# First feed-forward's gate/up with joined 512-column products over four PSUM banks

## The chip, the cores and the metric

The kernel runs on one core of one Trainium2 chip. The metric is the time of one execution on the device in microseconds (us), the lower the better.

## What is computed

Two transformer-like blocks follow each other. The first block works on 256 tokens of 1024 features: a mixer, then a gated feed-forward, then a small gate with a projected side input. The second block has two layers with conditioned norms; their scales and shifts come from a condition vector times a large matrix (`ada_w`). The stretch that matters here is the feed-forward of the first block, and beside it the condition product:

```python
h = rmsnorm(x, ffn_pre_norm[i])
f = (jax.nn.silu(h @ w_ffn_gate[i]) * (h @ w_ffn_up[i])) @ w_ffn_down[i]
x = x + rmsnorm(f, ffn_post_norm[i])

mod = jax.nn.silu(cond) @ w + b        # w is ada_w of either layer, for two conditions
```

Gate and up have 2816 columns each (22 tiles of 128). The same feed-forward stands in both layers of the second block, with the weights `ffn_w_gate_up` and `ffn_w_down`.

## The kernel before

Products are computed to more than the precision of one pass: every weight and every activation is split into a rounded high part and the low part that is left. With activations `xh`, `xl` (two halves of one tile, `xhl`) and weights `wh`, `wl`, a product is the sum of three matmuls: high by high, high weight by low activation, low weight by high activation.

Weights stream in units of 512 KB (`raw`, four slots). A unit passes four stations. SyncE's queue (SP) starts its transfer (`load`, L399) once GpSimd has finished with the unit four before it. ScalarE writes the high part `wh` (`high`, L649). GpSimd (POOL) writes the low part `wl` (`low`, L559). TensorE (PE) multiplies (`features`). Two units are one step, and a step of a gate/up phase gives one tile of gate and one tile of up. So there are 22 steps, numbered 0 to 21 below.

The gate/up phase of the first block is called `gu`. Its step alternates between pair 0 (bank 0) and pair 1 (bank 1); gate and up share a bank, 256 columns each. For every one of the 8 feature tiles, of both outputs, `three` (L1083 to L1085) issues three matmuls of 256 columns. After a step, ScalarE takes the silu of the gate (`sil`, L895), VectorE multiplies it by the up half (`ft`, L1770) and so frees the banks, ScalarE writes the high part `fh` (L899), and VectorE the low part `fl` (L1774), which it announces with the semaphore `f_lo`. ScalarE makes the high parts of the next weights (`high_step`) after `fh`, both units of a step one behind the other.

Beside this, VectorE computes the condition product row by row (`condition`, L1621 and L1624: two passes over a row tile of 1024, one per condition vector). The condition vectors lie in banks 2, 3, 5 and 6 at that time. VectorE does a step's rows at the head of that step, ahead of the wait for its silu. In the first 14 steps (`GU_LOOP` = 7 turns of a hardware loop, two slots for row tiles) a step has one row. In the last 8 steps, which are unrolled, steps of pair 0 have two rows and steps of pair 1 have one (`GX_ROWS`; four slots). The row tiles (512 KB each, `load_ada`, L429) are started by SP too, in one queue with the weights and in a fixed order: in the loop two units, a row, two units, a row; in the last steps a unit, then unit and row by turns. A row's transfer waits until VectorE has used up the row that lay in its slot (`ada_used`, counted by L1624), and whatever stands behind it in SP's queue waits with it.

The last layer's gate/up phase, `gu1`, is of the same size (256 tokens, 22 steps), has no condition rows beside it, and is written with joined products. There `joined` multiplies `wh` by `xh` and `xl` side by side, 512 columns into a whole bank (L1089), and `wl` by `xh`, 256 columns into the bank's first half (L1090). Such a step fills two banks, 0 and 1 or 2 and 3. Its results are in two halves that must be added: ScalarE copies the second halves of both banks to SBUF (`sf`, L891), VectorE adds them to the first halves (L1767), and then silu and the rest follow. ScalarE's order differs too: behind the copy it makes the high part of the first unit of the step after next (`high_half`), and that of the second unit behind `fh`.

The phase `dn` (down) follows `gu`, with three products of 256 columns in banks 0 and 1 and three condition rows to each pair of outputs. Bank 4 (`rstd_ps`) and bank 7 (`sums_ps`, `acc_ps`, and the last piece of the side projection, `PP_BANKS`) are used around `gu`, not in it; `take_pp` (L872) copies that piece out of bank 7 during step 0.

```python
def joined(o, wa, wb, k):
    nc.tensor.matmul(o, wa, xhl[:, :, k, 0:SEQ], start=k == 0, stop=False, skip_group_check=True)
    return nc.tensor.matmul(o[:, SEQ:2 * SEQ], wb, xh[:, k, 0:SEQ], ...)
```

Of the kernel before, what the change touches and what calls it, by code (L numbers as in the profile page):

```python
# [10 lines left out]
ALU = mybir.AluOpType  # L11
# [96 lines left out]
ADA_WOVEN = {"out": (1, 2, 0, 2), "gu": (1, 2, 2, 2 * GU_LOOP), "gx": (3, 4, 2 + 2 * GU_LOOP, 3 * (PH["gu"].iters - GU_LOOP))}  # L108
OUT = (1, 3, 0, 2, 4, 5, 6, 7)
GX_ROWS = ((0, 1), (2,))  # L110
JOINED = ('gu1',)
IN_U = (0, 1, 4, 5, 2, 3, 6, 7)
_at = sum(ADA_WOVEN["gx"][2:])
for _n, _per, _slots in (("dn", 3, 3), ("gu0", 2, 2), ("dn0", 3, 2)):
# [35 lines left out]
def build(nc, wall, wada, cond, xin, pin, par, tab, tab_ret, tab_rope, tab_mask, rpb, out):  # L150
    with ExitStack() as ctx:
        sems = {}

        def S(name):
            if name not in sems:
                sems[name] = ctx.enter_context(nc.semaphore(name))
            return sems[name]
# [135 lines left out]
        def pair_banks(j, n, wide=False):  # L293

            if n == SEQ and wide:
                return ps[:, 2 * j:2 * j + 2, 0:SEQ]
            if n == SEQ:
                return ps[:, j, :].rearrange("p (a b) -> p a b", a=2)
            return ps[:, 2 * j:2 * j + 2, :]

        def tile_bank(j, o, n, wide=False):

            return ps[:, j, o * SEQ:o * SEQ + SEQ] if n == SEQ and not wide else ps[:, 2 * j + o, 0:n]
# [340 lines left out]
        def _(act):  # L644
# [236 lines left out]
            def gate_up(ph, n, f0):  # L881

                def body(i, ahead=0):
                    for j in range(2):
                        split = ph.name in JOINED
                        if j >= ahead and not split:
                            high_step(ph, i, j)
                        pair_done(act, ph, i, j)
                        act.wait_ge(S("f_lo"), i * 2 + (f0 + j + 1))
                        if split:  # L890
                            nc.scalar.activation(sf[:, :, j, SEQ:NT], ps[:, 2 * j:2 * j + 2, SEQ:NT], ACT.Copy)\  # L891
                                .then_inc(S(f"small_{ph.name}"), 1)
                            high_half(ph, i, j + 1, 0)
                            act.wait_ge(S(f"joined_{ph.name}"), i * 2 + (j + 1))
                        nc.scalar.activation(sil[:, j, 0:n], tile_bank(j, 0, n, split), ACT.Silu)\  # L895
                            .then_inc(S("silu_ready"), 1)
                        act.wait_ge(bank_free, i * 2 + (ph.pair0 + j + 3))
                        settled(act)
                        nc.scalar.activation(fh[n][:, i * 2 + j, :], ft[:, j, 0:n], ACT.Copy).then_inc(S("f_hi"), 1)  # L899
                        if split:  # L900
                            high_half(ph, i, j + 1, 1)
                if ph.name == "gu1":
                    second_step(ph)
                if ph.name != "gu0":
                    preload(ACT.Silu)
                body(0, 1)
                with act.Fori(1, ph.iters) as i:
                    body(i)
# [162 lines left out]
        def _(pe):  # L1071
# [5 lines left out]
            def banks_ready(ph, i, pair):  # L1077

                pe.wait_ge(bank_free, i * 2 + (ph.pair0 + pair + 1))
# [13 lines left out]
            def features(ph, n, a=xh, b=xl, ktiles=KT, fresh=None, wide=False, within=None, first=0):  # L1093


                def body(i):
                    for j in range(ph.body):
                        pair = j // ph.per_pair
                        if j % ph.per_pair == 0:
                            banks_ready(ph, i, pair)  # L1100
                        for half in range(2):
                            slot = unit_ready(ph, i, j, half)
                            k0 = 2 * HALF * (j % ph.per_pair) + HALF * half
                            for o in range(2):
                                c = slice(o * P, o * P + P)
                                if within and isinstance(i, int) and (i, j) == (0, 0) and (half, o) in within:
                                    within[half, o]()
                                for kk in range(min(HALF, ktiles - k0)):
                                    k = k0 + kk
                                    if fresh and o == 0 and pair == 0:  # L1110
                                        sem, n0, each = fresh
                                        pe.wait_ge(S(sem), n0 + each * (k + 1))
                                    if ph.name in JOINED:
                                        mm = joined(ps[:, 2 * pair + o, :], wh[:, slot, kk, c], wl[:, slot, kk, c], k)
                                        continue
                                    mm = three(tile_bank(pair, o, n, wide), wh[:, slot, kk, c], wl[:, slot, kk, c],
                                               a[:, k, 0:n], b[:, k, 0:n], k == 0 and (n == NT or wide or o == 0), k == ktiles - 1)
                            mm.then_inc(units_done, 1)
                if first:
                    body(1)  # L1120
                else:
                    run(pe, ph, body, ph.iters - 1 if within else 0)
# [408 lines left out]
        def _(dve):  # L1531
# [225 lines left out]
            def gate_up(ph, n, f0):  # L1757
                def body(i):
                    for j in range(2):
                        if ph.name == "gu" and isinstance(i, int):  # L1760
                            condition("gx", 0, 0, [3 * (i - GU_LOOP) + s for s in GX_ROWS[j]])
                        else:
                            condition(ph.name, i, j)
                        dve.wait_ge(S("f_lo"), i * 2 + (f0 + j + 1))
                        if ph.name in JOINED:
                            dve.wait_ge(S(f"small_{ph.name}"), i * 2 + (j + 1))
                            V.tensor_tensor(pair_banks(j, n, True), pair_banks(j, n, True), sf[:, :, j, SEQ:NT], ALU.add)\  # L1767
                                .then_inc(S(f"joined_{ph.name}"), 1)
                        dve.wait_ge(S("silu_ready"), i * 2 + (f0 + j + 1))
                        V.tensor_tensor(ft[:, j, 0:n], sil[:, j, 0:n], tile_bank(j, 1, n, ph.name in JOINED), ALU.mult)\  # L1770
                            .then_inc(bank_free, 1)
                        dve.wait_ge(S("f_hi"), i * 2 + (f0 + j + 1))
                        f1 = bass.ds(i * 2 + j, 1)
                        V.tensor_tensor(fl[n][:, f1, :].rearrange("p a b -> p (a b)"), ft[:, j, 0:n],  # L1774
                                        fh[n][:, f1, :].rearrange("p a b -> p (a b)").bitcast(F32),
                                        ALU.subtract).then_inc(S("f_lo"), 1)
                run(dve, ph, body, ph.iters - GU_LOOP if ph.name == "gu" else 0)
# [432 lines left out]
```

## Time and profile before

| | |
|---|---|
| three runs | 1431.72, 1435.49, 1435.63 us (median 1435.49) |
| the profiled execution | 1431.83 us, of which the span is 1430.0 us |
| PE busy | 1391.8 us (97%) |
| PE weight loads | 1229.0 us (86%) |
| GpSimd busy | 845.2 us (59%) |
| VectorE busy | 749.9 us (52%) |
| ScalarE busy | 617.3 us (43%) |
| mean traffic with HBM | 156 GB/s |

Times in the rows are counted from the start of the span. Phase `gu` runs from 141.2 to 269.4 us, `dn` from there to 333 us, and `gu1` from 1231 to 1357 us. The columns of a timeline row are the start, the length, the engine, the line with its operation and tiles, and in brackets how long the engine had been idle and what released it. Matmuls overlap, so that the distance between two starts is the rate and the length is not.

### The profile page before, as it was taken

To read this page: it belongs to the slowest core of one execution; us is meant where nothing else is said; L and a number is where in the kernel's file an instruction comes from. 1 tells how busy PE (TensorE), PEld (TensorE's weight loads), DVE (VectorE), ACT (ScalarE), POOL (GpSimd) and SP (SyncE) were. 2 spreads that over 40 slices of the span, in tenths; PEclk is the share of its full clock that TensorE was granted. 3 is DMA by queue.
4 is the path that set the end of the run, shared out by engine and by line. 5 is a ranking of instruction groups with operands and counts; after the bars stand their busy time and mean duration, and the time that the engine had idled before them with its cause. 6 is when DMAs were issued, how large, how long until landed. Compare 5 with 4: busy or idle time off the path is not lost.

```text
span 1430.0 us, 24910 instructions
## 1 busy us (share of the span) xinstructions
PE 1391.8 (97%) x8774; PEld 1229.0 (86%) x8774; DVE 749.9 (52%) x1350; ACT 617.3 (43%) x997; POOL 845.2 (59%) x420
## 2 busy tenths in 40 slices
PE   9999999999999998899999999999999999999998
PEld 8999999999888887687888888888888788888897
DVE  4987457655634556637655655432514383444411
ACT  5566544444524444624323223322331365555552
POOL 5756888897374576132444444544465443688895
PEclk9999999999899999999999999999999999999999
DMA  7744678894232222033655556553393101455563
GB/s 250 252 156 155 243 281 305 290 322 146 82 92 86 74 74 74 17 102 105 204 194 202 177 192 219 178 185 134 93 243 97 44 18 62 140 184 185 186 211 103
DMA packets 82988, 227.28 MB, mean 159 GB/s; under 512 B 23664, under 2 KB 29040, under 8 KB 82672
## 3 DMA queue, kind: packets, MB, share of 16 engines
q1 hardware_dynamic: 82480, 224.91, 46.9%
q10 hardware_dynamic: 448, 1.57, 0.4%
q8 instruction: 37, 0.61, 0.2%
q14 instruction: 23, 0.19, 0.0%
HBM read 222.26 MB, written 1.05 MB: 156 GB/s over the span
## 4 chain that ended last, share of the span: by engine, by line
PE 42%; issue 32%; POOL 21%; DVE 4%; DVEq 1%; ACT 1%; POOLq 0%; ACTq 0%
POOL wl L559 18%; PE ps L1083 7%; PE ps L1085 7%; PE ps L1084 7%; PE ps L1089 6%; PE ps L1090 3%; DVE ps L1808 2%; PE ps L1170 2%; PE ps L1184 1%; PE ps L1160 1%; PE ps L1161 1%; PE ps L1162 1%; PE ps L1472 1%; POOL xhl L579 1%; PE ps L1398 1%
## 5 line engine op out<-in xcount | busy, mean ns | idle before, releaser
L559 POOL TENSOR_TENSOR wl<-raw,wh 128x1024 fp32r<-128x1024 f32 x310 | 747.4, 2432 | 519.7 <-ACT wh L649 519.4
L1083 PE MATMUL ps<-xhl,wh 128*128 128x256 f32 (+1 forms) x1376 | 460.2, 334 | 6.9 <-POOL wl L559 1.8
L1084 PE MATMUL ps<-xhl,wh 128*128 128x256 f32 (+1 forms) x1376 | 454.8, 331 | 0.0
L1085 PE MATMUL ps<-xhl,wl 128*128 128x256 f32 (+1 forms) x1376 | 454.8, 331 | 0.0
L649 ACT ACTIVATE wh<-raw 128x1024 fp32r<-128x1024 f32 x310 | 321.1, 1054 | 273.7 <-PE ps L1085 187.8
L1083 PEld LDWEIGHTS ps<-xhl,wh 128*128 128x128 f32 x1376 | 262.3, 191 | 39.1 <-POOL wl L559 4.3
L1085 PEld LDWEIGHTS ps<-xhl,wl 128*128 128x128 f32 x1376 | 262.3, 191 | 23.9
L1084 PEld LDWEIGHTS ps<-xhl,wh 128*128 128x128 f32 x1376 | 262.4, 191 | 22.7
L1083 PE MATMUL ps<-fh,wh 128*128 128x256 f32 (+1 forms) x528 | 168.8, 320 | 0.6 <-POOL wl L559 0.6
L1085 PE MATMUL ps<-fh,wl 128*128 128x256 f32 (+1 forms) x528 | 168.6, 319 | 0.0
L1084 PE MATMUL ps<-fl,wh 128*128 128x256 f32 (+1 forms) x528 | 168.6, 319 | 0.0
L1089 PE MATMUL ps<-xhl,wh 128*128 128x512 f32 x352 | 125.1, 400 | 1.2 <-DVE xhl L1582 0.8
L1751 DVE SCALAR_TENSOR_TENSOR h<-ps,mod,h 128x256 f32<-128x256 f32 x48 | 20.3, 478 | 169.6 <-PE ps L1085 169.6
L1083 PEld LDWEIGHTS ps<-fh,wh 128*128 128x128 f32 x528 | 99.3, 188 | 9.1 <-POOL wl L559 1.0
L1085 PEld LDWEIGHTS ps<-fh,wl 128*128 128x128 f32 x528 | 99.3, 188 | 8.1
L1084 PEld LDWEIGHTS ps<-fl,wh 128*128 128x128 f32 x528 | 99.3, 188 | 8.0
L895 ACT ACTIVATE sil<-ps 128x256 f32<-128x256 f32 (+1 forms) x66 | 29.9, 452 | 161.1 <-PE ps L1085 161.1
L1090 PE MATMUL ps<-xhl,wl 128*128 128x256 f32 x352 | 98.8, 281 | 0.0
L1770 DVE TENSOR_TENSOR ft<-sil,ps 128x256 f32<-128x256 f32 (+1 forms) x66 | 33.6, 510 | 104.3 <-ACT sil L895 104.3
L1774 DVE TENSOR_TENSOR fl<-ft,fh 128x256 f32 (+2 forms) x66 | 57.9, 878 | 49.9 <-ACT fh L899 49.9
L1089 PEld LDWEIGHTS ps<-xhl,wh 128*128 128x128 f32 x352 | 66.1, 188 | 19.0 <-DVE xhl L1582 1.4
L1621 DVE SCALAR_TENSOR_TENSOR unread<-ada_late,ps 128x1024 bf16<-128x1024 f32 x56 | 68.3, 1219 | 11.3 <-DMA ada_late<-wada 7.5
(230 smaller groups left out, 1885.8 us busy)
## 6 DMA issues: line engine op xcount, KB each, us to landing
raw<-wall SPq DMA_DIRECT2D x310, 512.0 KB, 4.1
ada_late<-wada SPq DMA_DIRECT2D x56, 512.0 KB, 3.3
ada<-wada SPq DMA_DIRECT2D x40, 512.0 KB, 5.5
bias<-rpb SPq DMA_DIRECT2D x16, 256.0 KB, 7.4
sww<-qk SPq DMA_DIRECT2D x16, 128.0 KB, 2.4
h<-xin SPq DMA_DIRECT2D x1, 1024.0 KB, 6.4
csb<-cond SPq DMA_DIRECT2D x1, 1024.0 KB, 6.5
h<-xin SPq DMA_DIRECT2D x2, 512.0 KB, 5.4
```

The costliest lines, as they stand in the source:

```text
L559: nc.gpsimd.tensor_tensor(wl[:, slot, :, :], raw[:, slot, :, :], wh[:, slot, :, :].bitcast(F32), ALU.subtract).then_inc(lo_ready, 1)
L649: nc.scalar.activation(wh[:, slot, :, :], raw[:, slot, :, :], ACT.Copy).then_inc(hi_ready, 1)
L895: nc.scalar.activation(sil[:, j, 0:n], tile_bank(j, 0, n, split), ACT.Silu)\
L1083: nc.tensor.matmul(o, wa, xa, start=start, stop=False, skip_group_check=True)
L1084: nc.tensor.matmul(o, wa, xb, start=False, stop=False, skip_group_check=True)
L1085: return nc.tensor.matmul(o, wb, xa, start=False, stop=stop, skip_group_check=True)
L1089: nc.tensor.matmul(o, wa, xhl[:, :, k, 0:SEQ], start=k == 0, stop=False, skip_group_check=True)
L1090: return nc.tensor.matmul(o[:, SEQ:2 * SEQ], wb, xh[:, k, 0:SEQ], start=False, stop=k == KT - 1, skip_group_check=True)
L1170: nc.tensor.matmul(ps[:, bank, 0:SEQ], filler[:, 0:P], filler, start=True, stop=True, skip_group_check=True)
L1621: V.scalar_tensor_tensor(junk, unit, 1.0, both[0], ALU.mult, ALU.mult, accum_out=mod_flat[:, at_, 0]).then_inc(S("ada_half"), 1)
L1770: V.tensor_tensor(ft[:, j, 0:n], sil[:, j, 0:n], tile_bank(j, 1, n, ph.name in JOINED), ALU.mult)\
L1774: V.tensor_tensor(fl[n][:, f1, :].rearrange("p a b -> p (a b)"), ft[:, j, 0:n], fh[n][:, f1, :].rearrange("p a b -> p (a b)").bitcast(F32) ...
```

## The change

The list of phases with joined products gets `gu`. Its pair 0 then uses banks 0 and 1, and pair 1 banks 4 and 7, since 2, 3, 5 and 6 hold the condition vectors. As 4 and 7 are no neighbours, the copy to `sf` and the addition are made in two instructions for pair 1, of 256 columns each, and in one for pair 0. PE waits for the last `take_pp` before it first writes pair 1.

```diff
-JOINED = ('gu1',)
+JOINED = ('gu', 'gu1')
...
+        def joined_parts(ph, j):
+
+            if ph.name == "gu" and j:
+                return [(0, 1, ps[:, 4:5, :]), (1, 2, ps[:, 7:8, :])]
+            return [(0, 2, ps[:, 2 * j:2 * j + 2, :])]
+
+        def joined_bank(ph, j, o):
+
+            return ps[:, 4 + 3 * o, :] if ph.name == "gu" and j else ps[:, 2 * j + o, :]
...
                         if split:
-                            nc.scalar.activation(sf[:, :, j, SEQ:NT], ps[:, 2 * j:2 * j + 2, SEQ:NT], ACT.Copy)\
-                                .then_inc(S(f"small_{ph.name}"), 1)
+                            for a, b, banks in joined_parts(ph, j):
+                                ins = nc.scalar.activation(sf[:, a:b, j, SEQ:NT], banks[:, :, SEQ:NT], ACT.Copy)
+                            ins.then_inc(S(f"small_{ph.name}"), 1)
                             high_half(ph, i, j + 1, 0)
                             act.wait_ge(S(f"joined_{ph.name}"), i * 2 + (j + 1))
...
                             banks_ready(ph, i, pair)
+                            if ph.name == "gu" and pair:
+                                pe.wait_ge(S("pp_taken"), 4)
...
-                                        mm = joined(ps[:, 2 * pair + o, :], wh[:, slot, kk, c], wl[:, slot, kk, c], k)
+                                        mm = joined(joined_bank(ph, pair, o), wh[:, slot, kk, c], wl[:, slot, kk, c], k)
...
                             dve.wait_ge(S(f"small_{ph.name}"), i * 2 + (j + 1))
-                            V.tensor_tensor(pair_banks(j, n, True), pair_banks(j, n, True), sf[:, :, j, SEQ:NT], ALU.add)\
-                                .then_inc(S(f"joined_{ph.name}"), 1)
+                            for a, b, banks in joined_parts(ph, j):
+                                ins = V.tensor_tensor(banks[:, :, 0:n], banks[:, :, 0:n], sf[:, a:b, j, SEQ:NT], ALU.add)
+                            ins.then_inc(S(f"joined_{ph.name}"), 1)
```

The silu and the product `ft` read their banks through `joined_bank`. By the same list, ScalarE's order in `gu` becomes that of `gu1`, and the first `high_step` of `dn` goes, because the last step of `gu` has made those units.

## Rows read from the trace of the kernel before

**Rows 1.** Busy time by stretch: first steps of gu, last 8, gu1; engines, clock, DMA.
```profile
147.10:222.10 75.00, 75.00 (x627) 75.00 (x627) 42.36 (x78) 35.63 (x52) 61.96 (x27) 1.00 0.72 259
222.10:269.35 47.25, 46.81 (x384) 46.02 (x383) 37.34 (x64) 22.39 (x32) 37.33 (x16) 1.00 0.92 326
1243.90:1357.00 113.10, 113.10 (x642) 98.00 (x641) 49.31 (x60) 63.71 (x100) 99.16 (x41) 1.00 0.55 185
```
**Rows 2.** Timeline of ScalarE in gu: take_pp, silu of steps 0, 13 and 21.
```profile
143.70 0.58 ACT L872 ACTIVATE ppo<-ps 128x512 f32<-128x512 f32 x1
...
147.25 0.38 ACT L895 ACTIVATE sil<-ps 128x256 f32<-128x256 f32 x1 [1.46 <-PE ps L1085]
...
222.21 0.39 ACT L895 ACTIVATE sil<-ps 128x256 f32<-128x256 f32 x1 [2.39 <-PE ps L1085]
...
269.49 0.38 ACT L895 ACTIVATE sil<-ps 128x256 f32<-128x256 f32 x1 [1.52 <-PE ps L1085]
```
**Rows 3.** Timeline of ScalarE in gu1: one step, and the same copy 11 steps later.
```profile
1289.89 0.60 ACT L891 ACTIVATE sf<-ps 128x512 f32<-128x512 f32 x1 [1.88 <-PE ps L1090]
1290.39 1.05 ACT L649 ACTIVATE wh<-raw 128x1024 fp32r<-128x1024 f32 x1
1291.34 0.38 ACT L895 ACTIVATE sil<-ps 128x256 f32<-128x256 f32 x1
...
1292.62 1.04 ACT L649 ACTIVATE wh<-raw 128x1024 fp32r<-128x1024 f32 x1
...
1352.09 0.60 ACT L891 ACTIVATE sf<-ps 128x512 f32<-128x512 f32 x1 [1.90 <-PE ps L1090]
```
**Rows 4.** Timeline of GpSimd and VectorE in the same step of gu1.
```profile
1291.52 4.94 POOL L559 TENSOR_TENSOR wl<-raw,wh 128x1024 fp32r<-128x1024 f32 x2 [0.69 <-ACT wh L649]
...
1290.53 0.70 DVE L1767 TENSOR_TENSOR ps<-ps,sf 128x512 f32<-128x512 f32 x1 [1.97 <-ACT sf L891]
1291.74 0.42 DVE L1770 TENSOR_TENSOR ft<-sil,ps 128x256 f32<-128x256 f32 x1 [0.52 <-ACT sil L895]
1292.87 1.33 DVE L1774 TENSOR_TENSOR fl<-ft,fh 128x256 f32 x1 [0.70 <-ACT fh L899]
```
**Rows 5.** Timeline of VectorE in gu's loop: the low part of step 6.
```profile
183.50 0.43 DVE L1774 TENSOR_TENSOR fl<-ft,fh 128x256 f32 x1 [0.70 <-ACT fh L899]
```
**Rows 6.** Timeline of SP's queue: a row tile, then a weight unit behind it.
```profile
186.62 0.33 SPq L429 DMA_DIRECT2D ada<-wada  x1
187.48 2.18 SPq L399 DMA_DIRECT2D raw<-wall  x2
```
**Rows 7.** Landing of raw units, from issue: that at 187.48; gu1; gu's last 8 steps.
```profile
DMA to landing us min/median/max: 4.8/4.8/4.8
...
DMA to landing us min/median/max: 3.0/3.2/3.4
...
DMA to landing us min/median/max: 4.1/5.6/7.6
```
**Rows 8.** Timeline of VectorE in gu's last steps: 17 to 19.
```profile
248.14 1.21 DVE L1621 SCALAR_TENSOR_TENSOR unread<-ada,ps 128x1024 bf16<-128x1024 f32 x1
...
253.13 0.42 DVE L1770 TENSOR_TENSOR ft<-sil,ps 128x256 f32<-128x256 f32 x1
254.13 0.43 DVE L1774 TENSOR_TENSOR fl<-ft,fh 128x256 fp32r<-128x256 f32 x1 [0.58 <-ACT fh L899]
254.47 1.22 DVE L1621 SCALAR_TENSOR_TENSOR unread<-ada,ps 128x1024 bf16<-128x1024 f32 x1
...
257.99 0.42 DVE L1770 TENSOR_TENSOR ft<-sil,ps 128x256 f32<-128x256 f32 x1 [1.03 <-ACT sil L895]
258.99 1.20 DVE L1774 TENSOR_TENSOR fl<-ft,fh 128x256 fp32r<-128x256 f32 x1 [0.58 <-ACT fh L899]
```
**Rows 9.** Lines by shape over gu: count, busy and mean of GpSimd's low parts.
```profile
L559 POOL TENSOR_TENSOR wl<-raw,wh 128x1024 fp32r<-128x1024 f32 x43 | 102.7, 2409 | 23.0 <-ACT wh L649 23.0
```
**Rows 10.** Timeline of PE where dn's second step (step 1) begins.
```profile
275.94 0.39 PE L1083 MATMUL ps<-fh,wh 128*128 128x256 f32 x1 [0.42 <-POOL wl L559]
```

More of the change, by code:

```diff
@@ L890, in body @@
                         if split:
-                            nc.scalar.activation(sf[:, :, j, SEQ:NT], ps[:, 2 * j:2 * j + 2, SEQ:NT], ACT.Copy)\
-                                .then_inc(S(f"small_{ph.name}"), 1)
+                            for a, b, banks in joined_parts(ph, j):
+                                ins = nc.scalar.activation(sf[:, a:b, j, SEQ:NT], banks[:, :, SEQ:NT], ACT.Copy)
+                            ins.then_inc(S(f"small_{ph.name}"), 1)
                             high_half(ph, i, j + 1, 0)
                             act.wait_ge(S(f"joined_{ph.name}"), i * 2 + (j + 1))
-                        nc.scalar.activation(sil[:, j, 0:n], tile_bank(j, 0, n, split), ACT.Silu)\
+                        nc.scalar.activation(sil[:, j, 0:n], joined_bank(ph, j, 0)[:, 0:n] if split else tile_bank(j, 0, n), ACT.Silu)\
                             .then_inc(S("silu_ready"), 1)
@@ L1766, in body @@
                             dve.wait_ge(S(f"small_{ph.name}"), i * 2 + (j + 1))
-                            V.tensor_tensor(pair_banks(j, n, True), pair_banks(j, n, True), sf[:, :, j, SEQ:NT], ALU.add)\
-                                .then_inc(S(f"joined_{ph.name}"), 1)
+                            for a, b, banks in joined_parts(ph, j):
+                                ins = V.tensor_tensor(banks[:, :, 0:n], banks[:, :, 0:n], sf[:, a:b, j, SEQ:NT], ALU.add)
+                            ins.then_inc(S(f"joined_{ph.name}"), 1)
                         dve.wait_ge(S("silu_ready"), i * 2 + (f0 + j + 1))
-                        V.tensor_tensor(ft[:, j, 0:n], sil[:, j, 0:n], tile_bank(j, 1, n, ph.name in JOINED), ALU.mult)\
-                            .then_inc(bank_free, 1)
+                        up_ps = joined_bank(ph, j, 1)[:, 0:n] if ph.name in JOINED else tile_bank(j, 1, n)
+                        V.tensor_tensor(ft[:, j, 0:n], sil[:, j, 0:n], up_ps, ALU.mult).then_inc(bank_free, 1)
                         dve.wait_ge(S("f_hi"), i * 2 + (f0 + j + 1))
```

## Prediction

> **What bounds the kernel now.** The page's busy shares come first: PE is busy 97% of the span, so a change pays only where it takes time off PE or off a wait of PE. The busy time by stretch then shows phase `gu` in two parts [rows 1]. In the first, PE never idles at the full granted clock, with VectorE busy 42.4 of 75 us. In the last 8 steps VectorE is busy 37.3 of 47.25 us. ScalarE's silu marks the end of each step [rows 2]: steps 1 to 13 take (222.21 - 147.25) / 13 = 5.766 us each, and the last 8 take 269.49 - 222.21 = 47.28 us, which is 1.15 us more than 8 x 5.766. This excess is PE waiting for weights that VectorE has held up: two rows stand before `ft`, `ft` before `fh`, and `fh` before the next high parts. I then read the timelines of ScalarE, VectorE, GpSimd and SP side by side, for one step each of `gu` and of `gu1`, which is already what `gu` is to become.
>
> **PE's part.** In `gu1` the copies at 1289.89 and 1352.09 are 11 steps apart [rows 3], so a joined step takes 5.655 us, with no idle PE [rows 1]. Per step 5.766 - 5.655 = 0.111 us goes, over 22 steps 2.4 us. Joined products save little: a 512-column matmul in place of two of 256 takes the same columns through the array. The Trainium skill, "TensorE: Matmul & The Clock Gate", "Back-to-back issue gap", gives N / 2.4 + 2.5 ns for a matmul of N columns, by which a joined tile would save 2.5 ns and 352 tiles 0.9 us; the rows differ (7 ns a tile) and decide. If everything else fitted, the stalls could go too: 2.4 + 1.15 in `gu`, and up to 1 us where `dn` begins, in all some 4.5 us.
>
> **VectorE's part, one step.** In `gu1` the copy starts at 1289.89, some 0.13 us after the step's end T. The addition starts 0.64 later, `ft` 1.21 after the addition, `fl` 1.13 after `ft`, and `fl` ends at 1294.20, T + 4.4 [rows 3, 4]. In `gu` today the silu follows T directly, and `fl` ends near T + 2.1 (183.93 in step 6 [rows 5]). `fl` is slow in `gu1` (1.33 against 0.43 us) because GpSimd works at that time; it ends 0.2 after GpSimd's first unit (1291.52 + 2.47). So it is ruled by that unit's end. A row, 2.5 us, follows `fl` and so ends 2.3 us later than now, or more.
>
> **What this does in SP's queue.** A row's transfer waits until an older row is used up, and weights stand behind it. One turn of that chain covers two steps:
> - end of `fl`, one row, issue of the row's transfer: 186.62 - 183.93 = 2.69 [rows 5, 6]
> - to the issue of the unit behind it: 0.86 [rows 6]
> - to its landing: 4.8 [rows 7]; I take 4.7, since neighbours are slightly shorter
> - ScalarE starts the high part (0.1, estimated), GpSimd starts 1.13 after that (1291.52 - 1290.39 [rows 3, 4])
> - low part 2.41 [rows 9], end of `fl` 0.3
>
> Together 12.2 us, against 11.53 for two steps now and 11.31 for PE alone when joined. Today the chain isn't closed: 187.48 + 4.8 lands about 1 us before the step ends after which ScalarE reads it [rows 6, 7], and the high part is asked for only behind `fh`. The change delays the landing by 2 to 3 us and asks for this unit 0.7 us sooner. Started at T + 4.4, the chain falls back 0.9 us every two steps: `fl` ends at T + 5.3, then T + 6.2, and from step 6 on unit 0 comes later than T + 5.65, when PE needs it. Steps 6, 8, 10 and 12 stall by about 0.3, 0.8, 0.8 and 0.8 us. First 14 steps: -14 x 0.111 + 2.7 = **+1.2 us**.
>
> **The last 8 steps.** Two steps of VectorE, without any wait for PE: two rows 4.99 (248.14 to 253.13), addition to `ft` 1.21, `ft` to `fl` 1.00, `fl` 0.34; one row 2.5, two additions to `ft` 1.28 (1.21 plus 0.07 for the second short one), `ft` to `fl` 1.00, `fl` 1.0 [rows 4, 8]. The sum is 13.3 us; now it is 11.98 with 1.03 of idle in it [rows 8], and PE joined wants 11.31. So VectorE becomes the bound. From the end of step 13: `fl` ends at 6.7 (the loop's lag), rows 4.99, addition to `ft` 1.21, which is 12.9 for `ft` of step 14. Step 18's `ft` is two turns later, 26.6. From it to the end of step 21: 0.88 to the second high part (1292.62 - 1291.74), 1.13 and 2.41 for GpSimd, 0.1 to PE, then half a step 2.83 and one step 5.655, which is 13.0. Together 52.5 us against 47.28: **+5.2 us**.
>
> **Start of dn.** Now PE starts its step 1 at 275.94 [rows 10] where 269.35 + 5.766 would be 275.1, a stall of 0.8 (the table load of ScalarE stands before those high parts), and some 0.2 in step 0. After the change, `ft` of step 20 is 5.9 behind its step's end; 4.5 more gives 10.4, or 4.75 into `dn`, where PE wants that half at 2.85: 1.9 us. The second step then fits. **+0.8 us**. `dn` keeps PE full after that, so nothing is given back.
>
> **Edits that cost nothing.** PE's wait for the last `take_pp`: that ends at 144.3 [rows 2], while pair 1 begins near 147. It would cost only if step 0 were 3 us shorter. The two copies in place of one lie in ScalarE's idle time (1.9 us before each copy [rows 3]), about 0.1 us later; they are in the 1.28. No table load is added. Banks 4 and 7 have no other reader in the phase. The weights of `dn` keep their place in SP's queue.
>
> **Sum.** +1.2 + 5.2 + 0.8 = +7.2 us. On the profiled execution, 1431.83, this is 1439.0. That one lies low: two of the three runs are at 1435.5. Against the median, 1435.49, it is 1442.7, and I predict **1442 us**. A difference of under 0.3% (4.3 us) can't be told from none.
>
> **Bounds.** The unknown that weighs most is the landing of the unit behind the row. From below, units in `gu1` land in 3.2 us with no row beside them [rows 7]: the chain is then 10.7, the loop gains its 1.55 us, `fl` of step 13 ends at 4.7, and the last steps cost 3.2: in all +2.5. From above, in the last steps the median is 5.6 [rows 7], and units now released together may do as badly: the chain is 13.1, the loop costs some 6, in all +12.5. I take 4.7, the nearest in place and in order of issue. Additions of 256 columns may take 0.2 more or less a turn, 0.6 us either way.
>
> **Rivals.**
> *A, the queue's chain doesn't bind, the last steps do.* The loop keeps its gain: +2.5 to +4, 1438 to 1439.5. For it: the chain is over PE's pace by only 0.9 in 12.2. Against: every term but one is from a row of this phase.
> *B, not slower: the additions vanish in VectorE's idle time.* VectorE idles 33 of 75 us in the loop and 10 of 47 in the last steps [rows 1], and the first unit's high part is now made ahead of VectorE's work, so only the second unit hangs on `ft`. `ft` may come until T + 3.95: 5.65 + 2.83 less 0.88, 1.13, 2.41 and 0.1. If it does, all stalls go: -4.5, 1431. This decides at `fl`: it holds if `fl` takes 0.43 and not until GpSimd's unit ends, and rows and additions overlap. Against: `fl` waits in all of `gu1`, and in the last steps 13.3 is over 11.31 even with short `fl` (12.7).
> *C, the queue is worse.* Unit, row and unit leave together and land as in the last steps: +12.5, 1448.
> *D, the change doesn't do what it says* (PE doesn't speed up in `gu`, its banks 4 and 7 being far apart): another +2.4; little speaks for it, and it is in the range.
>
> **How the numbers follow.** Forecast 0.52, A 0.22, B 0.13, C (with D) 0.13. Faster by over 0.3% needs all of B: 0.08. Within 0.3%: the rest of B, nearly all of A: 0.26. Slower: 0.66. The range takes in the forecast, A, and C to its own value: 1434 to 1448.
>
> **What would show it.** Right: PE's step 5.65 us in steps 1 to 5; then idle ScalarE before the first high part, released by the transfer of `raw`; `fl` ending 6 us and more behind its step; VectorE without idle from step 14 on, 13.3 us for two steps; PE stalls on GpSimd's `wl` in even steps; phase `gu` near 134.5 us, not 128.2. Wrong: a `gu` phase of 125 us, `fl` of 0.43 us, or ScalarE never waiting for `raw` in the loop. The prediction fails if units land in under 4 us behind a row, or if VectorE does its rows while it now waits.

## The result, and the profile after

The changed kernel takes 1444.32 us (median of 4 runs, 1443.28 to 1446.99), the kernel before beside it 1433.97. The ratio is 1.0078, with a 95% interval of 1.0061 to 1.0095: slower by about 11 us. The forecast, 1442, has the sign and nearly the size. But the growth was forecast at 7.2 us, and the sum under it was right in one part and wrong by a factor of five in another, as the steps show.

The profiled execution took 1444.73 us, of which the span is 1442.9. First the page's busy times (us, share of the span, instructions).

```profile
PE 1394.0 (97%) x8422; PEld 1211.6 (84%) x8422; DVE 773.4 (54%) x1383; ACT 629.4 (44%) x1030; POOL 846.3 (59%) x420
```

Little can be read there: PE's share is the same, and VectorE has the additions more and ScalarE the copies. The lines that tell more are the busy time by stretch, with the same columns as [rows 1], for the two parts of `gu`.

```profile
147.10:228.00 80.90, 74.56 (x418) 63.48 (x416) 54.96 (x93) 43.20 (x71) 62.36 (x26) 1.00 0.68 234
228.00:280.45 52.45, 47.98 (x257) 40.15 (x256) 43.49 (x76) 25.25 (x43) 38.28 (x16) 0.97 0.77 286
```

PE, which before was never idle in the first part, is idle for 6.3 of 80.9 us, and in the second for 4.5 of 52.5. The end of each step is read from PE's timeline (start of the step's last matmul plus 0.12 us), and gives the length of every step in us:

| step | before | after | forecast |
|---|---|---|---|
| 0 to 3, each | 5.76 | 5.65 | 5.655 |
| 4 | 5.76 | 6.33 | 5.66 |
| 6 | 5.76 | 6.71 | 5.95 |
| 8 | 5.76 | 7.24 | 6.45 |
| 10 | 5.76 | 7.86 | 6.45 |
| 12 | 5.76 | 7.61 | 6.45 |
| 5, 7, 9, 11, 13, each | 5.76 | 5.56 to 5.65 | 5.655 |
| 15 | 5.76 | 9.72 | (not by step) |
| 16, 18, 20 | 6.07, 6.19, 6.23 | 5.84, 6.80, 7.60 | (not by step) |
| 0 to 13, sum | 80.6 | 86.5 | +1.2 on before |
| 14 to 21, sum | 47.29 | 52.44 | 52.5 |

So the first 14 steps lost 5.8 us where 1.2 was forecast, and the last 8 lost 5.15 where 5.2 was. The start of `dn` lost 0.6 (from `gu`'s end to `dn`'s last matmul 64.3 us, before 63.7). Together 11.6 of the 12.9 us between the two spans; 0.2 lie ahead of `gu` and the rest after `dn`, where nothing was changed, and both are of the size by which executions differ.

What the engines wait for in `gu`, from the view of waits (engine, operation, line, what it waited for: us in total, times, longest):

```profile
ACT wh L659 <- DMA raw<-wall: 23.1, 13, 3.3
ACT sil L906 <- DVE ps L1781: 18.8, 14, 3.5
...
PE ps L1100 <- POOL wl L569: 10.1, 9, 1.9
```

In `gu` of the kernel before the first of these lines reads 1.3 us, once. ScalarE now stands 23 us in all in front of weights that haven't landed. One turn of the loop's chain can be followed on four engines, from the low part of step 4 to that of step 6. Columns as in [rows 2].

```profile
175.93 1.32 DVE L1788 TENSOR_TENSOR fl<-ft,fh 128x256 f32 x1 [0.70 <-ACT fh L910]
...
179.94 0.33 SPq L439 DMA_DIRECT2D ada<-wada  x1
180.80 0.92 SPq L409 DMA_DIRECT2D raw<-wall  x2
...
186.45 1.06 ACT L659 ACTIVATE wh<-raw 128x1024 fp32r<-128x1024 f32 x1 [2.80 <-DMA raw<-wall]
...
187.59 4.93 POOL L569 TENSOR_TENSOR wl<-raw,wh 128x1024 fp32r<-128x1024 f32 x2 [2.30 <-ACT wh L659]
...
188.93 1.30 DVE L1788 TENSOR_TENSOR fl<-ft,fh 128x256 f32 x1 [0.70 <-ACT fh L910]
```

And how long the two units issued at 180.80 and 181.40 took to land, then all units of the loop (174 to 223 us; for the units of its loop from 174 us on, the kernel before reads 3.2/4.2/5.1):

```profile
DMA to landing us min/median/max: 5.6/5.9/6.2
...
DMA to landing us min/median/max: 4.1/5.6/6.6
```

Term by term against the forecast: end of `fl` (177.25) to the row's transfer 2.69 (2.69), row to unit 0.86 (0.86), unit to the start of its high part 5.65 (4.7 + 0.1), high part to GpSimd 1.14 (1.13), and to the end of `fl` 2.64 (2.71). One turn is 12.98 us, later ones up to 13.4 (step 6 to step 12: 39.6 us for three turns, 13.2 each), where 12.2 was forecast. Every term is right but one: the landing of the first unit behind the row. In the loop's six turns it is 5.8, 4.9, 5.6, 5.9, 5.9 and 4.1 us, and the turns that begin with the first five of them last 13.25, 12.37, 12.99, 13.34 and 13.36: their length follows the landing.

### The profile page after: what moved, and what is told of

It reads as the page before. It is cut to its first block, busy times and chain, and to the rows that moved or that the text cites. A ratio compares the mean times of both kernels' runs of the same rounds, so it can differ in the third digit from the quotient of the medians.

```text
span 1442.9 us, 24293 instructions
## 1 busy us (share of the span) xinstructions
PE 1394.0 (97%) x8422; PEld 1211.6 (84%) x8422; DVE 773.4 (54%) x1383; ACT 629.4 (44%) x1030; POOL 846.3 (59%) x420
## 4 chain that ended last, share of the span: by engine, by line
PE 40%; issue 32%; POOL 21%; DVE 4%; ACT 1%; DVEq 1%; DMA 0%; POOLq 0%; ACTq 0%
POOL wl L569 18%; PE ps L1094 7%; PE ps L1095 7%; PE ps L1096 7%; PE ps L1100 5%; PE ps L1101 3%; DVE ps L1822 2%; PE ps L1197 1%; PE ps L1173 1%; PE ps L1174 1%; PE ps L1175 1%; PE ps L1485 1%; PE ps L1183 1%; PE ps L1411 1%; PE ps L1432 1%
## 5 line engine op out<-in xcount | busy, mean ns | idle before, releaser
L1094 PE MATMUL ps<-xhl,wh 128*128 128x512 f32 (+1 forms) x1024 | 360.3, 352 | 5.5 <-DVE xhl L2007 1.4
L1095 PE MATMUL ps<-xhl,wh 128*128 128x512 f32 (+1 forms) x1024 | 355.2, 347 | 0.0
L1096 PE MATMUL ps<-xhl,wl 128*128 128x512 f32 (+1 forms) x1024 | 355.1, 347 | 0.0
L1100 PE MATMUL ps<-xhl,wh 128*128 128x512 f32 x704 | 251.8, 402 | 12.1 <-POOL wl L569 10.5
L1094 PEld LDWEIGHTS ps<-xhl,wh 128*128 128x128 f32 x1024 | 195.0, 190 | 36.8 <-POOL wl L569 3.3
L1096 PEld LDWEIGHTS ps<-xhl,wl 128*128 128x128 f32 x1024 | 194.6, 190 | 24.1
L1095 PEld LDWEIGHTS ps<-xhl,wh 128*128 128x128 f32 x1024 | 195.0, 190 | 22.4
L1101 PE MATMUL ps<-xhl,wl 128*128 128x256 f32 x704 | 197.9, 281 | 0.0
L1100 PEld LDWEIGHTS ps<-xhl,wh 128*128 128x128 f32 x704 | 132.9, 189 | 49.3 <-POOL wl L569 13.9
L1101 PEld LDWEIGHTS ps<-xhl,wl 128*128 128x128 f32 x704 | 133.6, 190 | 0.0
L1788 DVE TENSOR_TENSOR fl<-ft,fh 128x256 f32 (+2 forms) x66 | 66.0, 1000 | 49.9 <-ACT fh L910 49.9
```

Source lines behind the costliest of these rows:

```text
L1094: nc.tensor.matmul(o, wa, xa, start=start, stop=False, skip_group_check=True)
L1095: nc.tensor.matmul(o, wa, xb, start=False, stop=False, skip_group_check=True)
L1096: return nc.tensor.matmul(o, wb, xa, start=False, stop=stop, skip_group_check=True)
```

## Experiments

Each ratio below is to runs of the kernel before on the same chip, whose medians there were 1432.35 (first four), 1431.73 (next four) and 1431.51 (last four). Two executions of one kernel differ by up to 0.6%, so that the lengths in `gu` carry the verdicts. They are of one execution each, and can themselves differ by some 2 us by the pace of PE (last section). The changed kernel wasn't run again beside them, so that times are compared with its own only roughly.

### Is it SP's queue? The first unit ahead of the row

```diff
-  unit 0, unit 1, row 0, unit 2, unit 3, row 1          # one turn of the loop, as SP issues it
+  unit 1, unit 2, row 0, unit 3, unit 0 of the next turn, row 1
   (in the last 8 steps every unit moves one place ahead in the same way)
```

> The changed kernel with SyncE's queue reordered in gu: the first unit of every step is issued ahead of the row tile that it now stands behind, and only second units stand behind rows. Theory (the row's wait in the queue holds up the first unit): the even steps' stalls in the loop go, the first 14 steps take 14 x 5.655 = 79.2 us (86.5 in the changed kernel), fl of step 13 ends near 4.7 us behind its step, and the last 8 steps take 4.7 + 4.99 + 1.21 + 26.4 + 13.0 = 50.3 (52.4). Phase gu 129.5 us, the kernel 9 us under the changed one and 2 to 3 over the kernel before. Rival (units land late because the transfers are too many, in whatever order): the stalls stay within 1 us a pair of steps, and the time stays within 2 us of the changed kernel's.

Measured: 1434.55 us, ratio 1.0006 (0.9990 to 1.0021). Steps 0 to 15 all take 5.55 us with no idle PE; then 7.01, 7.39 and 7.54 in steps 16, 18 and 20. The last 8 steps take 49.8 us. In `gu` ScalarE no longer waits for a transfer, so the queue's chain is what cost the loop its time, and it is gone with an order in which the unit that is wanted next doesn't stand behind the row. The tail stays: VectorE has no idle time in it but for the short waits inside one step.

```profile
147.10:220.00 72.90, 72.90 (x423) 64.30 (x422) 55.12 (x96) 43.64 (x73) 63.72 (x27) 1.00 0.78 281
220.00:269.00 49.00, 45.38 (x254) 38.23 (x252) 40.69 (x72) 24.25 (x41) 36.72 (x16) 1.00 0.77 283
```

### Is it VectorE's load in the tail? One row a step throughout

```diff
-GU_LOOP = 7        # rows: 1, 1 for a pair of steps; then 2, 1 in the last 8 steps; 3 for a pair of outputs in dn
+GU_LOOP = 11       # rows: 1, 1 for all 22 steps; 4 for a pair of outputs in dn
```

> The changed kernel with one condition row in every step of gu, where the last 8 steps had three for two steps; the four rows moved go to dn, which has four to a pair of outputs and not three. SyncE's order in gu stays. Theory (the queue's chain bounds a pair of steps at 13.3 us as soon as a row stands in each): the last 8 steps go from VectorE's 13.1 to the queue's 13.3 a pair, gu stays near 139 us, and the kernel is within 2 us of the changed one. Rival (VectorE's work is what costs): four rows of 2.5 us less in gu, so that gu loses 5 us or more.

Measured: 1444.63, ratio 1.0079 (1.0052 to 1.0106). Nothing is gained in the time. In `gu` step 10 takes 9.30 us, steps 14, 16, 18 and 20 take 7.0 to 7.2 each, the last 8 steps 50.7 and all of `gu` 137.4 us, 1.5 less than in the changed kernel. `dn` gives it back: it takes 67.0 us and not 64.3, with PE idle for 2.3 us at 291.91, behind a unit for which ScalarE had waited 2.7 us. With the old order in SP's queue, and two slots for rows to the end of `gu`, the chain goes on through the last 8 steps and takes the place of VectorE's work: 12.6 to 12.8 us for two steps there.

### Both, and the kernel before with its rows moved

> Both edits together: first units ahead of rows in the queue, and one row in every step of gu, four to a pair in dn. Theory: VectorE needs 11.1 us for two steps and TensorE 11.31, so all 22 steps run at 5.655 us, gu takes 124.5 us against 128.1 in the kernel before; the start of dn gains another 0.5 to 1 us; the kernel is 3 to 4.5 us under the kernel before. Rival (VectorE's latency behind each step binds all the same, or ten transfers to a pair of outputs hold up dn): gu over 127 us, or dn over 66 us (63.4 before), and no gain.

> The kernel before, with its products of 256 columns, and the rows spread as in the two kernels above. It says what the spread is worth without joined products. Theory: the stalls of gu's last 8 steps (1.15 us) go, dn stays as it is or loses up to 1 us by its ten transfers: within 1.5 us of the kernel before, and 2 to 3 us over the kernel with both edits. Rival (the spread alone brings the gain, the joined products nothing): as fast as the kernel with both edits.

Measured: both together 1429.59, ratio 0.9978 (0.9964 to 0.9992); the kernel before with rows moved 1431.91, 0.9990 (0.9977 to 1.0003). In the first all 22 steps take 5.65 us; in the second 5.76. That is joined products with nothing against them: 2.3 us in `gu` and 2.3 us between the two medians. (The two differ in SP's order as well, but PE doesn't stall in either `gu`.) `dn` gained nothing, against what was expected: 64.3 us with both edits, 63.7 in the other. The version with both edits is a little faster than both kernels.

```profile
147.10:220.00 72.90, 72.90 (x414) 63.23 (x413) 56.09 (x96) 42.50 (x72) 62.38 (x27) 1.00 0.79 278
220.00:264.00 44.00, 44.00 (x251) 38.20 (x250) 33.69 (x59) 26.35 (x44) 37.27 (x17) 1.00 0.77 270
```

### Is it the landing, or SP's wait by itself? Rows of an eighth of the bytes

```diff
-sp.dma_start(ada_slot(name, s % slots), wada[row, :, :])
+sp.dma_start(ada_slot(name, s % slots)[:, 0:128], wada[row, :, 0:128])      # in gu only; VectorE reads two of them over and over
```

> The changed kernel with its SP order, but each condition row of gu transfers 128 of its 1024 columns (64 KB in place of 512 KB), and VectorE's two passes read two of them over and over, so they keep their 1.2 us each; the rest of the row is left out. Theory (the mis-sized term is the landing of the unit behind the row, 5.6 to 6.3 us, since two units and a row share the DMA engines): the unit then lands in 3.2 to 4 us, the chain is 7.5 + 3.7 = 11.2 us for two steps, under PE's 11.3; steps 0 to 13 take 5.55 to 5.7 us each, step 13 ends near 221.5. The last 8 steps stay with VectorE, some 50 us. In all 1434 to 1437. Rival (SP is held up by the row's wait, whatever the bytes): the chain stays at 13.2, step 13 ends near 227, 1442 to 1445.

Measured: 1432.82, ratio 1.0009 (0.9992 to 1.0025), just under the expected range. Steps 0 to 14 take 5.65 us each, and the last 8 take 50.0. SP's order and its waits are those of the changed kernel; only the bytes are gone. The row and the units behind it in one half of a turn, and then how long four units took to land, those two (4.0 and 4.7) and the two of the half before:

```profile
187.26 0.33 SPq L440 DMA_DIRECT2D ada<-wada  x1
188.12 0.92 SPq L409 DMA_DIRECT2D raw<-wall  x2
```

```profile
DMA to landing us min/median/max: 4.0/4.3/4.8
```

So the wait in the queue costs nothing as long as the first unit behind it lands in 4.0 us. This tells the two readings apart: it was the term "landing", not the order alone. Three landings now stand side by side, as medians: a unit alone 3.2 [rows 7], two units and 64 KB 4.3, two units and a whole row 5.9. An estimate comes from the changed kernel's own busiest stretch, where the DMA engines have no gap and move 418 GB/s (second line of the windows further down): 524 KB / 418 GB/s = 1.25 us a transfer, and 3.2 + 2 x 1.25 = 5.7.

Bytes aren't the whole of it. In the other half of each turn a row and two units leave in the same way (185.62 and 186.22 in the changed kernel), and those units land in 4.7 and 5.5. The kernel before has a like difference between the halves, 4.8 and 4.0 for the first unit (187.48 and 181.94). And the landing of the first unit in the changed kernel varies between turns that look alike, from 5.9 to 4.9 and, in the last, 4.1. Why stays open.

The Trainium skill, "SBUF — State Buffer", "The DMA setup-cost knee", gives 2 us plus bytes / 436 GB/s for a transfer. An estimate by that page, taken over all that leaves together, is 3.2 us for a unit alone, 4.6 for two and 64 KB, and 5.6 for three. The traces agree for the first two (3.2, 4.3), and for the third in the middle of what they show (4.8 to 6.3 for the median of two units behind a row).

### What do the additions cost?

```diff
-V.tensor_tensor(banks[:, :, 0:n], banks[:, :, 0:n], sf[:, a:b, j, SEQ:NT], ALU.add)
+V.tensor_tensor(banks[:, :, 0:8], banks[:, :, 0:8], sf[:, a:b, j, SEQ:SEQ + 8], ALU.add)      # in gu only
```

> The changed kernel, with VectorE's addition of the halves in gu cut to 8 columns; the rest of the sum is left out. Theory: the queue's chain doesn't contain the addition (the low part fl is ruled by GpSimd's first unit), so steps 0 to 13 stay as they are, 86.5 us, with 13.2 for two steps. In the last 8 steps, which VectorE bounds with 13.1 for two steps, an addition saves 0.6 us twice: 11.9, and the 8 steps take 48 to 49.5 us in place of 52.4. In all 1439.5 to 1441. Rival (the additions are the cost of the change): both parts get short, 1433 to 1436.

Measured: 1440.32, ratio 1.0042 (1.0023 to 1.0060). The loop keeps its stalls (85.7 us for 14 steps, 86.5 in the changed kernel). The last 8 steps take 51.6 us, not the 48 to 49.5 expected. In them two steps of VectorE take 264.93 - 252.35 = 12.58 us, where 11.9 was expected and the changed kernel has 13.09: of 1.0 us taken out from addition to `ft` only half is gained. The other half goes into `fl`, which takes 1.60 and not 1.08 us, as it still has to wait until GpSimd's unit ends:

```profile
252.35 0.18 DVE L1782 TENSOR_TENSOR ps<-ps,sf 128x16 f32<-128x16 f32 x1
...
258.41 1.60 DVE L1789 TENSOR_TENSOR fl<-ft,fh 128x256 fp32r<-128x256 f32 x1 [0.58 <-ACT fh L910]
...
264.93 0.18 DVE L1782 TENSOR_TENSOR ps<-ps,sf 128x16 f32<-128x16 f32 x1
```

So the additions are the smaller part of the cost. `gu` is shorter by 1.6 us only. The medians differ by more, some 4 us; where the rest lies isn't shown.

### What do joined products give by themselves? Hardly any rows

```diff
-V.scalar_tensor_tensor(junk, unit, 1.0, both[0], ...)
+V.scalar_tensor_tensor(junk[:, :, 0:8], unit, 1.0, both[0][:, :, 0:8], ...)      # both passes; unit of 16 columns; transfers of 128 columns; in gu only
```

> The changed kernel, with each condition row of gu cut to 128 columns of transfer and 16 columns of each VectorE pass; the rest of the rows is left out. Theory: neither the queue nor VectorE binds, PE is never idle in gu, 22 steps of 5.55 to 5.655 us, 122.1 to 124.5 us, against 22 x 5.76 = 126.7 for the kernel before with the same cut (next run). The difference of the two is the whole of what joined products give: 2.3 us at 0.353 us a tile, 4.6 at 0.347. About 1429 to 1430. Rival B (the change has another cost of its own, in fl or ScalarE's order): PE is still idle in places, over 1431. Rival D (no gain on PE): as the next run.

> The kernel before, with the rows of gu cut as in the run ahead; the rest of the rows is left out. Theory: 22 steps of 5.76 us, 126.7 us, against 128.0 with whole rows, so about 1432.5. That is the time against which the run ahead shows the gain of joined products by itself.

Measured: with joined products 1427.11, ratio 0.9967 (0.9952 to 0.9982); without 1429.17, 0.9974 (0.9963 to 0.9984); both under what was expected. All steps are alike, 5.55 and 5.76 us. So the change does on PE what it says (rival D falls), and in an empty `gu` it has no cost of its own that shows on PE (rival B's mechanism would be right there). The two phases differ by 4.7 us, the two medians by 2.1. Half of the 4.7 is the faster of PE's two paces (last section): at 5.655 us a step it would be 2.3. Against it stands a loss ahead of `gu`: between 131 and 139.5 us the first of the two profiles has PE at a mean granted clock of 0.68 and the second at 1.00, and `gu` begins 2.3 us later in the first.

### Why is `fl` slow? The product in PSUM

```diff
-V.tensor_tensor(ft[:, j, 0:n], sil[:, j, 0:n], up_ps, ALU.mult)
+V.tensor_tensor(joined_bank(ph, j, 1)[:, SEQ:NT], sil[:, j, 0:n], up_ps, ALU.mult)      # in gu; fh and fl read it there
+pe.wait_ge(S("f_lo"), i * 2 + (pair + 1))                                               # before PE's next use of the bank
```

> The changed kernel, with the product ft of gu written into the second half of the up bank in PSUM in place of SBUF (PE's next use of the bank then waits for fl, not for ft). VectorE's low part fl has then one operand in SBUF, not two. Theory (fl takes 1.3 us because, with two operands in SBUF, it stands behind GpSimd's low part, which reads SBUF too): fl takes 0.45 to 0.6 us in all of gu. One turn of the queue's chain falls from 13.2 to 12.3 us, steps 0 to 13 take some 83 us in place of 86.5, VectorE's two steps in the tail 12.45 in place of 13.1, so the last 8 steps some 49.8 in place of 52.4. In all 1437 to 1440. Rival (fl is long for another reason, or PE's new wait for fl binds): fl stays at 1.3 us, 1443 to 1447.

Measured: 1433.82, ratio 1.0007 (0.9993 to 1.0020), better than expected. The low parts in the steps of 147 to 228 us, grouped by line and shape (count, busy us, mean ns), in the changed kernel and then in this one:

```profile
L1788 DVE TENSOR_TENSOR fl<-ft,fh 128x256 f32 x13 | 12.5, 959 | 9.0 <-ACT fh L910 9.0
```

```profile
L1793 DVE TENSOR_TENSOR fl<-ps,fh 128x256 f32 x14 | 5.9, 424 | 9.2 <-ACT fh L913 9.2
```

In the changed kernel they take 0.42 to 1.42 us, long where GpSimd is at work; here all are short, although GpSimd works beside them as before. Steps 0 to 13 take 81.5 us (expected 83, changed kernel 86.5), one turn 12.0 (step 6 to step 12: 35.97 us for three) and the last 8 steps 48.3 (expected 49.8). A subtraction with both operands in SBUF waits for GpSimd's; with one of them in PSUM it doesn't. That alone took back 9.1 us in `gu`, and 10.5 between the medians. The Trainium skill, "SBUF — State Buffer", "Who interferes with whom", says that a VectorE instruction with two SBUF inputs contends with a GpSimd instruction that reads SBUF; by that rule, the traces agree (0.96 against 0.42 us in the mean). The forecast priced this wait rightly but took it as given.

### ScalarE's old order

```diff
-sf copy, high part of the first unit, sil, fh, high part of the second unit
+sf copy, sil, fh, high parts of both units                                   # in gu only
```

> The changed kernel, with ScalarE's order in gu as in the kernel before: both high parts of a step behind fh, none behind the copy. Theory: with copy and addition ahead of it, fh ends 2.85 us after a step's end, the high part 1.05 later, GpSimd's first low part starts at 4.0 and ends at 6.4, but PE wants the unit at 5.65: each step takes 6.5 to 6.6 us, gu some 143 us (139 in the changed kernel); fl is short, 0.43 us, since GpSimd is idle then. In all 1447 to 1452. Rival (what costs is fl being behind GpSimd's early unit, so the new order of ScalarE is the harm): fl short, the chain short, 1438 to 1441.

Measured: 1442.60, ratio 1.0071 (1.0045 to 1.0096): between the two expected ranges, and about where the changed kernel is. From step 2 on the loop's steps take 5.9 to 6.45 us each, 12.2 to 12.5 for two, not 13. My expectation had a slip that is worth seeing. The first unit is ready 6.5 us after the end of step s (183.82 for the rows below, ready at 190.3), but it serves step s + 2 and not s + 1. From the end of step s to that of step s + 2 it is then 6.5 + 5.65 = 12.15 us, 6.1 a step in the mean and not 6.5, however the two steps share it.

```profile
186.50 0.42 ACT L911 ACTIVATE fh<-ft 128x256 f32 x1 [0.58 <-DVE ft L1788]
186.82 1.99 ACT L659 ACTIVATE wh<-raw 128x1024 fp32r<-128x1024 f32 x2
...
187.94 4.78 POOL L569 TENSOR_TENSOR wl<-raw,wh 128x1024 fp32r<-128x1024 f32 x2 [1.34 <-ACT wh L659]
```

So neither order fits. With the old one ScalarE waits for a transfer for 0.4 us in all of `gu`, and `fl` takes 0.42 us in the loop, but GpSimd starts late; with the new one the queue's chain binds.

### The repairs combined

> The run with the first units ahead of the rows in SP's queue, and ft in the bank as well. Theory: the loop stays at PE's pace (5.55 to 5.655 us a step), and in the last 8 steps VectorE's two steps fall from 13.1 to 12.45 us, still over PE's 11.3: the 8 steps take 47 to 48 us in place of 49.8. In all 1431 to 1433, the kernel before being at 1431 to 1434. Rival (the tail isn't bound by VectorE's busy time): the 8 steps stay at 49.8 us, 1434.5.

> Units first, the rows of the last steps moved to dn, and ft in the bank. Theory: without ft in the bank this schedule already had PE idle for 1.5 us only in gu, so the shorter fl lies off the path and saves nothing but a part of that: 1428.5 to 1430.5, 0.1 to 0.3% under the kernel before. Rival (something of VectorE's late fl still costs in gu or in dn's start): 1427 or less.

Measured: units first with the product in the bank 1429.35, ratio 0.9982 (0.9969 to 0.9995), under the 1431 to 1433 expected; all three 1429.57, 0.9974 (0.9960 to 0.9988). In the first, steps 0 to 15 take 5.55 us, the last 8 steps 47.6 (expected 47 to 48), and steps 19 and 20 together 12.4 (expected 12.45): the tail is VectorE's, and shortens by what `fl` saves. In the second every step takes 5.65 us, as it did without the product in the bank: a shorter `fl` is worth nothing once it is off the path.

## Why the prediction was right, and where not

- **PE's part, right in size.** 5.655 was forecast for a step and 5.65 measured where nothing stalls, in steps 0 to 3 and in the two versions with rows moved and units first. Against the same layout of rows with three matmuls that was 2.3 us in `gu` and between the medians. Some runs took 5.55 a step, which no row had shown.
- **The chain in SP's queue, right as a mechanism, one term too small.** The landing of the unit behind the row was taken at 4.7 us, "the nearest in place and in order of issue". It measured 5.6 to 5.9 in four of the six turns, 4.9 and 4.1 in the other two. The row that I took, 187.48, has a second unit that was issued more than a microsecond behind the first, because GpSimd hadn't yet freed its slot (2.18 us for two [rows 6]). In the changed kernel SP is blocked at the row for so long that both units are free when it goes on (0.92 us for two), and three transfers leave together. That the second unit, close behind, is what delays the first is a reading only: no run varied it by itself. What a run did vary is the bytes of the rows, and with an eighth of them the unit lands in 4.0 us and the loop's stalls are gone. The prediction had named this as the upper bound ("units now released together may do as badly") and as rival C, with +6 for the loop: that was the case, +5.8. With 5.65 for 4.7 + 0.1 (4.8) the chain is 13.0 instead of 12.2 us, and since only what is over 11.3 us costs, 0.8 us more in it doubled the growth, and brought the stalls two steps earlier. A small misreading without effect: `fl` of step 6 ended at T + 2.3 before, not T + 2.1.
- **The last 8 steps, right to 0.1 us.** 52.5 forecast, 52.44 measured. The parts hold as well, counted from the end of step 13 (227.93): `fl` ends at 6.6 (6.7), two rows take 4.99 (4.99), `ft` of step 14 starts at 12.70 (12.9), that of step 18 at 39.4 (12.9 + 26.6 = 39.5), and the end of step 21 is another 13.04 later (13.0). Two small errors cancel: the first turn of VectorE, with a longer `fl` in it, takes 13.61 and the next 13.09, where 13.3 was forecast for each. The start was safe from the first error, as I read it (not tested): once PE stalls on the chain, the lag of `fl` behind its step is fixed by where PE stalls, however long the chain is. VectorE without a wait for PE, two steps apart:

```profile
253.10 0.69 DVE L1781 TENSOR_TENSOR ps<-ps,sf 128x512 f32<-128x512 f32 x1
...
260.19 1.08 DVE L1788 TENSOR_TENSOR fl<-ft,fh 128x256 fp32r<-128x256 f32 x1 [0.58 <-ACT fh L910]
...
266.19 0.69 DVE L1781 TENSOR_TENSOR ps<-ps,sf 128x512 f32<-128x512 f32 x1
```

  That is 13.09 us against the sum's 13.3.
- **Start of dn, right in the difference.** +0.8 forecast, +0.6 measured. PE is idle for 1.25 us there, not 1.9, and was so for 0.6 before, not 1.0. It lies in the second unit of its first step, and in a new wait for `ft` of 0.56 at its very start, which wasn't named:

```profile
281.08 0.36 PE L1094 MATMUL ps<-fh,wh 128*128 128x256 f32 x1 [0.56 <-DVE ft L1785]
...
284.86 0.39 PE L1094 MATMUL ps<-fh,wh 128*128 128x256 f32 x1 [0.69 <-POOL wl L569]
```

- **The total** is nearer to the forecast than its parts deserve. The loop cost what C said (+5.8), so that the growth by parts is 11.6 and not 7.2 us. C as a whole (+12.5) is what the profiled span shows (+12.9), and the medians show 10.4; I gave it 0.13. That 1442 is only 2.3 us off is in part luck: it was counted from a median of 1435.49, and the kernel before came out at 1433.97 beside the changed one.
- **Rival A** (the chain doesn't bind) falls with ScalarE's 23 us in front of `raw`, and with the units moved ahead of the rows, which took the loop's stalls away. **Rival B** (the additions vanish) hung on a short `fl` and on rows overlapping with additions. The product in the bank made `fl` short and took 9.1 us back in `gu`, though from step 6 on PE still stalls in nearly every second step. With the additions cut short the loop's stalls stayed.

## To carry to other kernels

When a change delays the point at which an in-order DMA queue goes on, count what has come free behind it in the meantime: it may all leave together, and land later than where transfers leave one by one (here the first unit mostly in 5.6 to 5.9 us, where 4.8 had been read). Sum the turn of such a chain, compare it with the period of the engine that should bound, and remember that only the excess costs, so that a term wrong by 0.8 us in 12 made the stalls nearly three times as long here. And before an addition is paid for on VectorE, look at what its operations wait for: here moving one operand out of SBUF, or one unit ahead of one row, was worth nearly the whole of what the change had cost.

## What the runs showed that I had not expected

**A joined tile has two paces.** The same pair of matmuls (512 and 256 columns, PE never idle, granted clock 1.00) took 0.353 us in some stretches and 0.347 in others: 5.655 or 5.55 us a step, 2.3 us over the phase. The pace holds for a whole stretch and changes, where it does, at a stall: the changed kernel's steps 0 to 3 ran at 5.65, and steps 13, 17 and 19, each behind a stalled one, at 5.55; with the first units ahead of the rows `gu` ran at 5.55 from its first step, with the rows moved as well at 5.65. In `gu1`, where no version differs, it was 0.353 in thirteen of the fourteen profiles and 0.347 in the one of units first with the product in the bank, 2.0 us over the phase. Three matmuls of 256 took 0.360 in `gu`, and in `dn` 0.356 in thirteen profiles and 0.360 in the one of units first. So the same instructions ran at either pace, and what chooses it stays open. It makes 2.3 us of `gu` in the run with units first, and two lengths of one phase should be compared at one pace.

**A stall in `gu` was followed by a stretch at half clock.** In step 15 SP's queue stood at the first row of the tail until the loop's last row was used up. PE was idle for 0.5 and 1.8 us, and then, with PE at work again since 239.20, the granted clock fell from 2.4 to 1.2 GHz until 243.8:

```profile
230.78 0.33 SPq L439 DMA_DIRECT2D ada<-wada  x1
231.17 0.42 SPq L409 DMA_DIRECT2D raw<-wall  x1
...
239.20 0.51 PE L1100 MATMUL ps<-xhl,wh 128*128 128x512 f32 x1 [1.78 <-POOL wl L569]
...
241.56 0.63 PE L1100 MATMUL ps<-xhl,wh 128*128 128x512 f32 x1
...
242.20 0.63 PE L1100 MATMUL ps<-xhl,wh 128*128 128x512 f32 x1
```

The two starts are 0.64 us apart, where 0.353 is usual. In the busy time by stretch the mean granted clock of those microseconds is the last but two of the numbers:

```profile
240.00:242.00 2.00, 2.00 (x10) 1.66 (x9) 0.97 (x3) 1.21 (x3) 2.00 (x1) 0.62 1.03 422
242.00:246.00 4.00, 4.00 (x20) 3.46 (x19) 3.52 (x8) 2.53 (x5) 3.09 (x3) 0.76 1.03 418
```

Step 15 took 9.72 us: 5.65, 2.3 of idle time, and about 1.8 for the half clock. It cost little in the end, since VectorE bounds this part anyway. The same happened with the additions shortened (10.07 in step 15), and in step 10 of the run with rows moved and SP's order kept (9.30); it didn't in `gu` of any other run, nor after the idle time of 1.93 us ahead of 203.36 in this one.
